# Two fused transformer blocks on one core: the order of the gated panels and the second value panel

## The reference

```python
h = rms_norm(x, norm_mix_g[l]) * (1.0 + sc1) + sh1
proj = h @ w_in[l]                                  # 2048 x 8192
u, q, k, v, ga, gb = jnp.split(proj, split_at, axis=-1)
y_ssm = s5_branch(u, ...)                           # ends: y = gelu(y); y * sigmoid(y @ w_glu + b_glu)
y_att = moba_attention(q, k, v, rel_bias)           # 8 heads of 128
merged = (jax.nn.sigmoid(ga) * (y_ssm @ w_proj_ssm[l])
          + jax.nn.sigmoid(gb) * (y_att @ w_proj_attn[l]))
x = x + g1 * (merged @ w_out[l])
```

## Time and profile before

| | |
|---|---|
| median of 3 runs | 3023.93 us (3023.45 to 3027.39) |
| the profiled execution, its own time | 3022.38 us |
| its span, first to last instruction | 3021.1 us |
| mean granted clock of PE, of full speed | 0.988 |
| PE busy | 2936.4 us (97%) |
| DVE busy | 2067.5 us (68%) |
| ACT busy | 1381.6 us (46%) |
| read from HBM | 624.68 MB, 208 GB/s over the span |

### The profile page before, as it was taken

One profiled execution on the slowest core, in us unless ns is written; L12 is line 12 of the kernel. 1 busy time (PEld: TensorE's weight loads), 2 busy tenths in 40 slices (PEclk: granted clock), 3 DMA queues, 4 the chain that ended last, 5 costly groups with the idle time before them and its releaser, 6 DMA issues.

```text
span 3021.1 us, 42836 instructions
## 1 busy us (share of the span) xinstructions
PE 2936.4 (97%) x17353; PEld 2545.8 (84%) x17353; DVE 2067.5 (68%) x2399; ACT 1381.6 (46%) x1692; POOL 255.5 (8%) x256
## 2 busy tenths in 40 slices
PE   5899999999999999999999999999999999999998
PEld 3688899888888888889999987778898888888886
DVE  6789978997777746556788776675557645555555
ACT  3334344444544434344556655554445444444443
POOL 6845520000000000000000000000000000000000
PEclk7999999999999999999999999999999999999999
DMA  9866798896677766664556665456555666566664
GB/s 339 311 192 202 208 301 279 292 344 225 209 263 250 245 190 184 198 188 160 176 172 185 189 189 154 155 158 192 188 183 169 191 187 188 194 189 193 190 189 152
DMA packets 303522, 631.70 MB, mean 209 GB/s; under 512 B 21872, under 2 KB 26384, under 8 KB 302752
## 3 DMA queue, kind: packets, MB, share of 16 engines
q1 hardware_dynamic: 298496, 618.74, 64.6%
q10 hardware_dynamic: 2800, 5.33, 0.5%
q0 software_dynamic: 2032, 4.90, 0.5%
HBM read 624.68 MB, written 4.21 MB: 208 GB/s over the span
## 4 chain that ended last, share of the span: by engine, by line
PE 88%; DVE 6%; DMA 3%; issue 2%; ACT 1%; SPq 0%; ACTq 0%; DVEq 0%
PE PS L1032 16%; PE PS L1048 14%; PE PS L1049 14%; PE PS L1050 14%; PE PS L1036 8%; PE PS L1019 6%; PE PS L1021 6%; PE PS L1020 6%; DVE wlo L1985 2%; DMA F<-in_w_ada 1%; DVE aacc L1974 1%; PE PS L830 1%; ACT whi L2518 1%; DVE F L1974 0%; DMA F<-in_w_proj_attn 0%
## 5 line engine op out<-in xcount | busy, mean ns | idle before, releaser
L1985 DVE TENSOR_TENSOR wlo<-raw,whi 128x1024 fp32r<-128x1024 f32 x858 | 1075.4, 1258 | 718.6 <-ACT whi L2518 717.9
L2518 ACT ACTIVATE whi<-raw 128x1024 fp32r<-128x1024 f32 x858 | 905.2, 1059 | 1089.1 <-PE PS L1050 554.8
L1048 PE MATMUL PS<-whi,R 128*128 128x512 f32 x2016 | 796.9, 395 | 5.9 <-DVE R L1486 5.4
L1049 PE MATMUL PS<-whi,R 128*128 128x512 f32 x2016 | 786.8, 390 | 0.0
L1050 PE MATMUL PS<-wlo,R 128*128 128x512 f32 x2016 | 786.4, 390 | 0.0
L1032 PE MATMUL PS<-R,whi 128*128 128x512 f32 x2048 | 516.2, 394 | 10.8 <-DVE R L1893 5.4
L1019 PE MATMUL PS<-R,whi 128*128 128x256 f32 x1792 | 514.0, 287 | 7.7 <-DVE wlo L1985 7.5
L1020 PE MATMUL PS<-R,whi 128*128 128x256 f32 x1792 | 509.5, 284 | 0.0
L1021 PE MATMUL PS<-R,wlo 128*128 128x256 f32 x1792 | 509.4, 284 | 0.0
L1048 PEld LDWEIGHTS PS<-whi,R 128*128 128x128 f32 x2016 | 379.3, 188 | 93.7 <-issue 5.8
L1050 PEld LDWEIGHTS PS<-wlo,R 128*128 128x128 f32 x2016 | 379.3, 188 | 80.4
(11 more groups left out here) (424 smaller groups left out, 1799.7 us busy)
## 6 DMA issues: line engine op xcount, KB each, us to landing
raw<-in_w_in SPq DMA_DIRECT2D x276, 512.0 KB, 4.1
raw<-in_w_ff SPq DMA_DIRECT2D x175, 512.0 KB, 4.4
raw<-in_w_ada SPq DMA_DIRECT2D x134, 512.0 KB, 5.4
raw<-in_w_mlp_up SPq DMA_DIRECT2D x128, 512.0 KB, 3.9
raw<-in_w_mlp_down SPq DMA_DIRECT2D x128, 512.0 KB, 4.4
F<-in_w_ff SPq DMA_DIRECT2D x81, 512.0 KB, 4.4
F<-in_w_ada SPq DMA_DIRECT2D x58, 512.0 KB, 5.8
raw<-in_w_out SPq DMA_DIRECT2D x53, 512.0 KB, 4.4
```

The source lines that it names most:

```text
L1048: pe.matmul(o, hi, whi[:, s, w], start=first, stop=False)
L1049: pe.matmul(o, lo, whi[:, s, w], start=False, stop=False)
L1985: v.tensor_tensor(wlo[:, i % SPN, :], words(j), whi[:, i % SPN, :].bitcast(F32), ALU.subtract).then_inc(lo_done, 1)
L2518: a.activation(whi[:, i % SPN, :], words(j), ACT.Copy).then_inc(hi_done, 1)
```

## The change

Both gated panels now stand ahead of v1: glu0 is units 120 to 123, glu1 124 to 127, v1 128 to 135. All else keeps its number. glu0 moves to banks 6 and 7, and since it no longer counts in the alternation, every later alternating panel changes sides. The tanh and the products are made at once, but their results stay in PSUM, and ACT rounds them only when v1's fourth unit is done (`first_half_read`), DVE's low parts follow. The heads 4 to 7 start at v1's end minus 3, 2, 1 and plus 6 ticks, instead of plus 2, 3, 4 and 11. `close_at` passes over the glu panels and v1.

```diff
@@ the list of panels
     for i in range(2):
         for name, c0 in (("q", 1024), ("k", 2048), ("v", 3072)):
+            if name == "v" and i:
+                for j in range(2):
+                    panel("glu", j, w2("w_glu"), 0, 8, j * 512, yg, lambda k: (yg_ready, k + 1), (ys_ready, j + 1))
             panel(name, i, w_in, 0, 16, c0 + i * 512, h, by_h, (evac_a[name], i + 1), name == "v")
-    for i in range(2):
-        panel("glu", i, w2("w_glu"), 0, 8, i * 512, yg, lambda k: (yg_ready, k + 1), (ys_ready, i + 1))
+    first_half_read = unit_done, len(unit_src) - 4
@@ banks
-    order = {id(x): n for n, x in enumerate(x for x in panels if x.name not in ("KV", "Q"))}
+    order = {id(x): n for n, x in enumerate(x for x in panels if x.name not in ("KV", "Q") and (x.name, x.i) != ("glu", 0))}
...
+        elif x.name == "glu" and x.i == 0:
+            x.bank = 6
@@ close_at
             x = panel_of[n]
-            if x.units < 8 or x.name in ("glu", "ps", "pa"):
+            if x.name == "glu" or (x.name, x.i) == ("v", 1):
+                n += 1
+                continue
+            if x.units < 8 or x.name in ("ps", "pa"):
                 return n, 7
@@ heads
-    HEAD_TICK = [end_of["v", i] + t for i in range(2) for t in (2, 3, 4, 11)]
+    HEAD_TICK = [end_of["v", 0] + t for t in (2, 3, 4, 11)] + [end_of["v", 1] + t for t in (-3, -2, -1, 6)]
@@ DVE, glu
-            if p == 0:
-                yield
+            yield
             v.wait_ge(glu_t, p + 1)
             for half in range(2):
-                if half and p == 0:
+                if half:
                     yield
...
-            if p == 0:
+            for e in range(8 - 3 * p):
                 yield
             v.wait_ge(glu_hi, 2 * p + 2)
@@ ACT, glu
             t.then_inc(glu_t, 1)
+            for e in range(9 - 3 * p):
+                yield
+            a.wait_ge(*first_half_read)
             for half in range(2):
-                if p == 0 and half == 0:
-                    yield
-                    yield
```

## The result

The changed kernel takes 3030.41 us (median of 22 runs, 3025.55 to 3033.66), the kernel before 3024.09 us in the same sets (22 runs, 3020.60 to 3027.39). The ratio is 1.0019, 95% interval 1.0013 to 1.0024: slower by 0.19%, some 6 us. The forecast was 3023.6 us and no difference.

What follows compares the result with a forecast made beforehand. DVE's backlog was taken to bound the stage: 1.8 us gained less 1.5 us of idle gives 0.3 us, so 3023.93 - 0.3 = 3023.6 us, no difference, range 3019.0 to 3029.0.

Steps and rivals of the forecast that it cites:

- Idle DVE after 547.8: DVE from tick 136's wlo through unit 163's: 1.5 us of idle waiting for loads, taken off a 1.8 us gain.
- lower end: Loads at 1.44 us each: DVE passes unit 163 at 631.3 us with no idle.
- upper bound: Loads at 1.55 us each: DVE passes unit 163 at 636.8 us, 5.4 us of idle, a loss of 3.6.
- Unit 139 may be rounded from 546.7: ACT's rounding ahead of tick 136: free from 546.7 us, so that tick's wlo on DVE begins at 547.8.
- 557 + 50x + 2.3: When DVE passes unit 163 if loads bind: 50 loads of x us from about 557, then a rounding and a wlo.
- What bounds the kernel: The stage ends on DVE's backlog, not PE's; the stall and half clock at ps0 offer 7.2 us, 0.24%.
- PE up to ps0: PE from unit 120 on: ps0 starts at 546.5 instead of 552.66 us, with about 0.4 us wait at head 5.
- DVE's balance: Tick 136 through unit 163's wlo: 83.55 us of DVE work for 70.15, passing at 631.4, at best 1.8 us earlier.
- Where PE stands: PE waits four times for the wlo of units 145 to 148, 5.6 us in all.
- Rival 2: Loads bind behind ps0: at 1.6 us each, 3030.0 us; chance 0.07 over 0.2% slower, 0.15 for 1 to 6 us.
- Rival 1: PE's stall at ps0 is the price: PE keeps 7.2 us less 0.4 at head 5, 3017.1 us; chance 0.12.
- Rival 3: Nothing moves at ps0: ys_ready comes late and PE waits as long at head 5, 3023 to 3026 us; chance 0.06.

Runs made afterwards that it cites:

- head 7 experiment: Changed kernel with head 7 started two ticks later (v1's end plus 8): 3028.42 us, ratio 1.0010 to the kernel before, stage 288.7 us.
- both quarters: Changed kernel with DVE working on, and loads bringing, only 256 of 1024 columns of w_ada pieces 80 to 107: 3015.74 us, ratio 0.9972.
- kernels with early pieces: Changed kernel with the fourth group closed at unit 128 again, so w_ada pieces keep their old ticks, in several variants: ratios 0.9983 to 1.0001.
- the close at 128 in bank 5: Changed kernel with the fourth group's close back at unit 128, sums in bank 5: 3019.30 us, ratio 0.9983; run again, 0.9986.
- bank 4: Changed kernel with the fourth group's close back at unit 128, its sums in bank 4 instead of bank 5: 3022.75 us, ratio 1.0001.

## Why the prediction was wrong

**The failed step** is "Idle DVE after 547.8. This is the unknown ... I take 1.5 us of idle, nearer the lower end". It was 7.3 us. The end then lies at 631.4 + 7.3 + 0.6 (work) = 639.3 us by the prediction's own sum; measured, 642.96 - 3.77 = 639.2. The mechanism, DVE's backlog returning PE's gain, was right, and the size of this term was off by 5.8 us, of the 6.3 us by which DVE's end was missed. Even the upper bound, 5.4, was too low. The term turned a forecast of no difference into a loss.

Of the 7.3 us, 2.2 are ACT's order at v1's end: the prediction took "Unit 139 may be rounded from 546.7" from PE alone and did not list what stood in ACT's queue there, though the copy of v1 moves with v1's end to just that point. The experiment that undoes it has 2.9 us less of DVE idle. 3.4 us are the three waits for roundings behind late loads, and 1.7 us are breaks of under 0.15 us each.

The prediction's own formula for loads shows the same from the other side. It had DVE through unit 163 at 557 + 50x + 2.3. The 557 stood on an issue of piece 84's load at 554.3; that was at 556.7, 2.4 us later, behind ACT's order. With 559.4 for 557, the measured 639.2 asks for x = 1.55 us: the rate of the earlier trace rows, which the prediction had as its upper bound. So the choice of the lower end cost 3.9 us of the miss (632.9 to 636.8), and the late start 2.4. This is a reckoning with one mean rate and not a measurement; what shows the start is the kernel with the copy of v1 later (2.8 us less through unit 163).

For the lower end the prediction argued that six full buffers cover 8.6 us; but it compared each bound with PE or with its own mean, and not the two with each other. They are 1 us apart, and here the two together were longer than either (137.6 and 138.6 alone, 140.5 together).

Point by point:
- *What bounds the kernel.* Right: the stage ends on DVE's results in both kernels, with the same 1.08 us wait ahead of the last turn, and PE's gain at ps0 is not the kernel's. Not said was that the loads are an equal bound.
- *PE up to ps0.* Right: 546.85 for 546.5. Head 5's wait was 0.3 us for 0.4, no clock loss, and ps0's second unit starts at 549.57 by the same reckoning, where the first takes 2.72 us instead of 4.5.
- *DVE's balance.* Right: 84.13 us of work for 83.55, and 14.2 us of idle ahead for "about 14". The wlo of units 145 to 148 is then 3.1 to 3.4 us later than forecast; 2.1 of that are there at unit 139.
- *Where PE stands.* Wrong in form: one wlo wait of 1.1 us for 5.6 in four, the rest at head 7's scores (2.36), a head's transposes (2.17) and a turn (2.30). By the stage of the head 7 experiment it makes no difference.
- *The loads.* Rival 2 is nearest to what happened, and its sign (DVE idle of more than 4 us behind 550 under ACT's waits for DMA) was seen. It gave DVE at 639.3 for 1.6 us a load and 3030.0 us in all. That this meets the measured 639.2 and 3030.4 is partly luck: it leaves out DVE's work, the equal bound, and the late start, and takes a slower single rate for both. It had 0.07 for over 0.2% and 0.15 below; the sign, if not the size, should have had more. That rate is not what the trace shows: from 572 to 604 us the loads run at 356 GB/s, 1.47 us each, with share 1.00, and from 604 to 643 at 327, 1.60 each, with idle engines in between. Ahead of that, up to 551.57, they run at 225 GB/s, since no pieces are due in the ticks 130 to 137. Room that was not used there was missing behind it. "DMA: Bandwidth & Descriptors" of the Trainium skill (Specifications) has about 358 GB/s as a core's limit from HBM. The stretch agrees with 356, but shorter stretches go above it (the last section). A mean rate answered how fast loads go, but not whether they are in time.
- *Rival 1*, PE's stall is the price: falls here, since ps0 came 5.8 us earlier and nothing was won; it is true only with both other bounds taken away (both quarters, 7.6 us for 7.2). The rule that the prediction took from the Trainium skill's "Perfetto Trace Analysis" (Optimization Strategy) speaks of the gaps within the regime at hand, where the most contended engine may be another. So it was here: the most busy engine of the span did not end this stage.
- *Rival 3* falls: 0.3 us at head 5. It is what happens in the kernels with early pieces, where head 5 or ps0 waits 0.9 to 7.0 us for `ys.lo`.

## What to carry to other kernels

A stall of the busiest engine is worth only what the stage's other bounds leave of it: 7.2 us here, of which nothing came. Before an order is changed, list what moves along with it, in every engine's list; here a helper that looks for a free tick put off 12 pieces of work by up to 8 units, from a stretch that had room for them, and that cost 7 to 10 us, while the order without it wins 4 to 5 by the medians and 1.5 to 2.8 by the stage (the close at 128 in bank 5; in bank 4 the median shows no gain). Where two bounds of a stage come out within a few per cent, don't take the larger one: allow for waits between them, and test by cutting each and both.

## What the runs showed of the hardware

The clock after a stand of PE is not told by the length of that stand. Windows of PE (us, busy, granted clock, DMA share, GB/s): the changed kernel behind its stand of 2.36 us; the kernel with the close at 128 behind its stands of 3.80 and of 3.18 us; the same kernel again, behind 3.80 us; bank 4, from within its stand of 6.99 us (which ends at 545.92) on.

```profile
573.00:576.40 3.40, 3.40 (x10) 0.50 0.99 315
```
```profile
541.80:545.40 3.60, 3.57 (x16) 1.00 0.95 336
548.60:552.00 3.40, 3.35 (x16) 1.00 0.98 352
```
```profile
543.50:546.90 3.40, 3.40 (x10) 0.50 1.03 407
```
```profile
541.70:551.90 10.20, 5.97 (x15) 0.50 0.97 360
```

Behind 2.36 us PE was at 1.2 GHz for a while, behind 3.80 and 3.18 us it stayed at 2.4, and behind the same 3.80 us it was at 1.2 in another execution. At half clock PE did 10 matmuls where it does 16. In the second profile of the kernel with the close at 128 this cost nothing: with the slow stretch ahead of it, the wait for `ys.lo` was 1.1 us instead of 3.2, and the stage is the shorter of the two (280.07 and 281.34 us). The loads went at 407 GB/s in one of these stretches, above the 365 of the earlier trace rows; the Trainium skill's "HBM Reference" (Specifications (TRN2)) has about 425 GB/s for a core that streams alone, which leaves room for it.
